# Moving the norm's squares on ScalarE and the last mixed group's activations on VectorE in a fused decoder layer

## The reference, cut to what matters

```python
h = h + jnp.concatenate([o_gdn, o_moba], axis=-1) @ w_o[i]
hn = rms_norm(h, ffn_norm[i])
h = h + (jax.nn.silu(hn @ w_gate[i]) * (hn @ w_up[i])) @ w_down[i]
```

## Time and profile before

| | us |
|---|---|
| median of 3 runs | 1311.7 |
| lowest and highest | 1311.44, 1312.51 |
| the profiled execution, its time | 1312.5 |
| the profiled execution, its span | 1310.8 |
| TensorE busy in it | 1302.5 |
| VectorE busy | 1025.2 |
| ScalarE busy | 704.7 |

### The profile page before, as it was taken

The page is one execution under the profiler, slowest core; times in us unless marked ns, Lnnn a source line. Parts: engine busy times, 40 slices in busy tenths (PEclk is TensorE's granted clock), DMA queues, the critical chain, the costliest instruction groups (busy, mean ns, idle before and its releaser), DMA issues.

```text
span 1310.8 us, 18558 instructions
## 1 busy us (share of the span) xinstructions
PE 1302.5 (99%) x6595; PEld 1076.9 (82%) x6595; DVE 1025.2 (78%) x1381; ACT 704.7 (54%) x937; POOL 53.7 (4%) x71
## 2 busy tenths in 40 slices
PE   9999999999999999999999999999999999999998
PEld 8788888887888887888888888888888888888887
DVE  6578886788586668889888988679888997968554
ACT  6576444543455565555555654445555555555643
POOL 4003000221000000000000000000000000000000
PEclk9999999999999999999999999999999999999999
DMA  8555554455434555665666556566666656556563
GB/s 271 177 174 164 159 147 129 145 149 152 144 119 145 177 177 164 205 211 184 194 198 207 192 193 216 185 211 184 198 205 209 190 182 209 193 178 208 193 199 139
DMA packets 126204, 238.37 MB, mean 182 GB/s; under 512 B 9711, under 2 KB 10786, under 8 KB 126138
## 3 DMA queue, kind: packets, MB, share of 16 engines
q1 hardware_dynamic: 126106, 237.48, 56.8%
q10 hardware_dynamic: 32, 0.01, 0.0%
HBM read 235.36 MB, written 2.10 MB: 181 GB/s over the span
## 4 chain that ended last, share of the span: by engine, by line
PE 98%; DVE 1%; ACT 0%; issue 0%; DMA 0%; DVEq 0%; ACTq 0%
PE pair L627 16%; PE pair L629 16%; PE pair L628 16%; PE pair L908 11%; PE pair L909 11%; PE pair L910 11%; PE bg L908 2%; PE bg L909 2%; PE bg L910 2%; PE bg L748 2%; PE bg L818 2%; PE bg L685 1%; PE bg L903 1%; PE bg L799 0%; PE bg L660 0%; DVE w_lo L1493 0%
## 5 line engine op out<-in xcount | busy, mean ns | idle before, releaser
L1493 DVE TENSOR_TENSOR w_lo<-raw,w_hi 128x1024 fp32r<-128x1024 f32 x442 | 531.8, 1222 | 179.2 <-ACT w_hi L1099 177.4
L1099 ACT ACTIVATE w_hi<-raw 128x1024 fp32r<-128x1024 f32 x401 | 417.1, 1055 | 250.5 <-PE pair L629 139.9
L627 PE MATMUL pair<-w_hi,xT_hi 128*128 128x512 f32 x780 | 314.6, 403 | 0.0
L629 PE MATMUL pair<-w_hi,xT_lo 128*128 128x512 f32 x780 | 305.0, 391 | 0.0
L628 PE MATMUL pair<-w_lo,xT_hi 128*128 128x512 f32 x780 | 304.4, 390 | 0.0
L629 PEld LDWEIGHTS pair<-w_hi,xT_lo 128*128 128x128 f32 x780 | 146.5, 188 | 31.5
L627 PEld LDWEIGHTS pair<-w_hi,xT_hi 128*128 128x128 f32 x780 | 146.9, 188 | 28.9
L628 PEld LDWEIGHTS pair<-w_lo,xT_hi 128*128 128x128 f32 x780 | 147.0, 188 | 27.4
L1373 ACT ACTIVATE w_hi<-raw 128x1024 fp32r<-128x1024 f32 x41 | 43.6, 1062 | 134.7 <-DVE raw L1823 134.7
L908 PE MATMUL pair<-w_hi,actT_hi 128*128 128x512 f32 x296 | 115.9, 392 | 0.0
L910 PE MATMUL pair<-w_hi,actT_lo 128*128 128x512 f32 x296 | 115.3, 389 | 0.0
(11 more groups left out here) (351 smaller groups left out, 1886.0 us busy)
## 6 DMA issues: line engine op xcount, KB each, us to landing
raw<-in_w_in_dram SPq DMA_DIRECT2D x112, 512.0 KB, 3.7
raw<-in_w_gate_dram SPq DMA_DIRECT2D x88, 512.0 KB, 4.6
raw<-in_w_up_dram SPq DMA_DIRECT2D x88, 512.0 KB, 4.5
raw<-in_w_down_dram SPq DMA_DIRECT2D x88, 512.0 KB, 4.8
raw<-in_w_o_dram SPq DMA_DIRECT2D x32, 512.0 KB, 3.9
raw<-in_w_ple_gate_dram SPq DMA_DIRECT2D x32, 512.0 KB, 4.1
raw<-in_w_ple_proj_dram SPq DMA_DIRECT2D x4, 512.0 KB, 4.1
h<-in_x_dram SPq DMA_DIRECT2D x3, 512.0 KB, 8.0
```

The source lines that it names most:

```text
L627: mm(banks[t][:], hi[:, ts], wh, start=first, stop=False)
L629: m = mm(banks[t][:], lo[:, ts], wh, start=False, stop=last)
L1099: f(w_hi[j % RING][:], raw[j % RING][:], ACT.Copy).then_inc(hi_ready, 1)
L1493: v.tensor_tensor(w_lo[j % RING][:], raw[j % RING][:], w_hi[j % RING][:].bitcast(F32), ALU.subtract).then_inc(lo_ready, 1)
```

## The change

`res_end` on ScalarE (the squares) is called later: for the first three `w_o` blocks two units into the next block, behind that step's `post("hA")`, and for the fourth block at step j = 3 of the first gate/up block, behind `post("hA", 7)`. ScalarE's rounding of group 7's forms is split off into `round_forms` and called at step j = 6; VectorE's whole part of group 7 (`post("hA", 7)`) is called at step j = 6 too, and behind it the sum of the squares. `res_end` loses its unused arguments. SyncE's, TensorE's and GpSimd's lists do not change.

```diff
--- before.py
+++ after.py
@@ -178,6 +178,7 @@
        + [("gate", MIXED[1]), ("up", MIXED[1])] + [("up", PLAIN[0])]
        + [("gate", MIXED[2]), ("up", MIXED[2])] + [("up", g) for g in PLAIN[1:]])
 assert len(SEQ) == 2 * UPB
+LAST_FORMS = SEQ.index(("up", MIXED[1])) - 2
 MIXED_END = SEQ.index(("up", MIXED[-1]))
 
 
@@ -1099,6 +1100,13 @@
                 f(w_hi[j % RING][:], raw[j % RING][:], ACT.Copy).then_inc(hi_ready, 1)
 
 
+            def round_forms(b, q):
+
+                act.wait_ge(form_ready, 4 * q + 1)
+                f(xT_hi[:, 2 * b, P:TOK], F_raw[:, 0, :], ACT.Copy)
+                act.wait_ge(form_ready, 4 * (q + 1))
+                f(F_hi[:, q, :, :], F_raw[:, 1:4, :], ACT.Copy).then_inc(form_rounded, 1)
+
             def post(step, b, half=None):
                 bk, i, use_n = where((step, b))
                 bh = heads(bk[:])
@@ -1136,10 +1144,8 @@
                         act.wait_ge(xg_ready, 2 * (q + 1))
                         f(xT_hi[:, 2 * b, 0:P], xg[:, 0, 0:P], ACT.Copy)
                         f(xT_hi[:, 2 * b + 1, :], xg[:, 1, :], ACT.Copy).then_inc(x_hi, 2)
-                        act.wait_ge(form_ready, 4 * q + 1)
-                        f(xT_hi[:, 2 * b, P:TOK], F_raw[:, 0, :], ACT.Copy)
-                        act.wait_ge(form_ready, 4 * (q + 1))
-                        f(F_hi[:, q, :, :], F_raw[:, 1:4, :], ACT.Copy).then_inc(form_rounded, 1)
+                        if b < UPB - 1:
+                            round_forms(b, q)
                         return
                     if step == "hA":
                         f(h1_raw[:], bk[:].rearrange("p (k t n) -> p k t n", k=2, t=NT)[:, :, 1, :], ACT.Copy).then_inc(h1_copied, 1)
@@ -1337,14 +1343,12 @@
                     f(mv[:, t, (b - 4) * CB:(b - 3) * CB], pair[n % 2][t][:], ACT.Copy,
                       scale=x_rs[:, t:t + 1]).then_inc(pair_free[n % 2], 1)
 
-            def res_end(last_unit, i, n):
-
-                wait_block(act, last_unit)
-                bno = (B_WO if i == 0 else B_DB) + n
-                wait_pair_read(act, bno)
+            def res_end(n):
+
+                wait_pair_read(act, B_WO + n)
                 for t in range(NT):
-                    f(junk[:], h[:, t, n * CB:(n + 1) * CB], ACT.Square, accum_out=h_ss[i][:, t, n:n + 1]).then_inc(h_sq, 1)
-                    act.wait_ge(h_sq, 8 * i + 2 * n + t + 1)
+                    f(junk[:], h[:, t, n * CB:(n + 1) * CB], ACT.Square, accum_out=h_ss[0][:, t, n:n + 1]).then_inc(h_sq, 1)
+                    act.wait_ge(h_sq, 2 * n + t + 1)
 
             for u in range(U_Z, U_GUA):
                 split(u + LEAD, u + LEAD)
@@ -1355,8 +1359,8 @@
                     z_end((u - U_Z) // UPB)
                 if U_WO - 2 * UPB <= u < U_WO and (u + 1 - U_MIX) % UPB == 0:
                     mix_end((u - U_MIX) // UPB)
-                elif U_WO <= u < U_GUA and (u + 1 - U_WO) % UPB == 0:
-                    res_end(u, 0, (u - U_WO) // UPB)
+                elif U_WO + UPB <= u and (u - U_WO) % UPB == 2:
+                    res_end((u - U_WO) // UPB - 1)
 
             def turned(n, kt):
 
@@ -1443,6 +1447,10 @@
                         for k in range(2):
                             for s in AT[u0 + j][k]:
                                 post(*s)
+                    if peeled and n0 == 0 and j == 3:
+                        res_end(3)
+                    if peeled and n0 == 0 and j == LAST_FORMS:
+                        round_forms(UPB - 1, len(MIXED) - 1)
                     if j == MIXED_END:
                         act.wait_ge(t_used, i * len(MIXED) + (m0 + len(MIXED)))
                         f(act_s[1][:], bg[0][:], ACT.Copy).then_inc(p1_copied, 1)
@@ -1783,16 +1791,12 @@
                     if n == 2 and j in (1, 5):
                         post("ba" if j == 1 else "gc", 0)
 
-            def res_end(last_unit, i, n):
+            def res_end(last_unit, n):
 
                 wait_block(dve, last_unit)
-                bno = (B_WO if i == 0 else B_DB) + n
                 for t in range(NT):
                     o = h[:, t, n * CB:(n + 1) * CB]
-                    v.tensor_tensor(o, o, pair[bno % 2][t][:], ALU.add).then_inc(pair_free[bno % 2], 1)
-                if n == 3:
-                    dve.wait_ge(h_sq, 8 * (i + 1))
-                    v.reduce_sum(h_s[i][:], h_ss[i][:], AX_X).then_inc(h_sum, 1)
+                    v.tensor_tensor(o, o, pair[(B_WO + n) % 2][t][:], ALU.add).then_inc(pair_free[(B_WO + n) % 2], 1)
 
             for u in range(U_Z, U_GUA):
                 split(u + LEAD, u + LEAD)
@@ -1802,7 +1806,7 @@
                 if u < U_MIX and (u + 1 - U_Z) % UPB == 0:
                     z_end((u - U_Z) // UPB)
                 if U_WO <= u < U_GUA and (u + 1 - U_WO) % UPB == 0:
-                    res_end(u, 0, (u - U_WO) // UPB)
+                    res_end(u, (u - U_WO) // UPB)
 
             def turned(n, kt):
                 for q in range(2):
@@ -1917,7 +1921,13 @@
                     if peeled:
                         for k in range(2):
                             for s in AT[u0 + j][k]:
-                                post(*s)
+                                if s != ("hA", UPB - 1):
+                                    post(*s)
+                    if peeled and n0 == 0 and j == LAST_FORMS:
+                        post("hA", UPB - 1)
+                    if peeled and n0 == 0 and j == 6:
+                        dve.wait_ge(h_sq, 8)
+                        v.reduce_sum(h_s[0][:], h_ss[0][:], AX_X).then_inc(h_sum, 1)
                     if j == MIXED_END:
                         p1 = act_s[1]
                         dve.wait_ge(p1_copied, i + (n0 + (2 if n0 else 0) + 1))
```

## The result

The median is 1314.47 us (22 runs, 1312.05 to 1315.53) against 1311.74 us before (22 runs on the same chips, 1310.95 to 1312.66). The ratio is 1.0019 with a 95% interval of 1.0013 to 1.0024: slower by 2.7 us. The interval leaves out 1, so the loss is real, and the bound of 0.2% lies inside it (by the two medians alone the difference is 0.21%). The profiled execution took 1314.79 us, with a span of 1313.1 us.

A forecast was written before the change was run, and what follows sets the result against it. TensorE was taken to bound the kernel, losing time only in a wait for VectorE's w_lo and a slow clock. From 1311.4, adding 1.49 + 0.2 and 0.9 of clock loss gave 1314.0 us, range 1311.6 to 1315.4.

The forecast's parts named there:

- the bound of 0.2%: Smallest difference that a measurement of this kernel was said to tell from no change: 2.6 us, upper limit 1314.3.
- block 4's squares: Ahead of G3, leaving lets G5's difference start 0.51 us earlier; ahead of G7's rounding, VectorE gets a new 2.0 us wait.
- the forms: Behind G9's w_lo they cost 2.68 us; G11's w_lo ends 1.49 later, TensorE waits 0.4 at G10, 2.5 at G11.
- 530.17: Time until which TensorE would have waited at G11 in the kernel before without a clock fall, 1.13 us before 531.30.
- 1.49 + 0.2: Time added without the clock: 1.49 us for the later w_lo of G11 and 0.2 for block 3.
- the clock's: Slow TensorE clock behind the wait ahead of G11: 0 to 1.7 us, taken as 0.9.
- 1311.4: Base of the sum: the kernel before without a clock fall, which is its fastest run.
- rival 1: Slower by over 0.2%: the clock falls fully behind the wait ahead of G11, 1314.8 us; chance 0.40.
- Block 3: Its moved squares delay the w_lo of G-2: 0.2 us taken, bounds nothing and 0.4.
- Behind the pairs: VectorE's lateness up to G15's w_lo has a cover of 0.3 us: costs nothing, at worst 0.2.
- Rival 2: Squares don't hold G7 up, G11's w_lo ends 0.5 us earlier: 1310.9 without, 1312.6 with clock loss; chance 0.11.
- Rival 3: Faster: w_lo of G8 and G11 come in time, all waits and the slow clock go, 1308.4 us; chance 0.07.

The follow-up runs named there:

- Run 1: Changed kernel with group 7's forms left between the w_lo of G6 and G7, so only the squares are moved: 1312.91 us.
- run 3: Changed kernel with block 4's squares one unit later, behind G7's rounding: 1312.99 us.
- run 2: Changed kernel with all squares back at the block ends as before, so only group 7's forms and their sum are moved: 1312.95 us.
- run 5: Kernel before with eight matmuls of unused product keeping TensorE busy in its wait ahead of G8: 1311.55 us.
- run 9: Changed kernel with the squares of blocks 1 to 3 back at the blocks' ends: 1314.27 us.
- run 7: Run 3 with group 6's transposes behind G0 instead of in the middle of G1: 1312.36 us.
- run 4: Changed kernel with nine matmuls of unused product keeping TensorE busy in its wait ahead of G11: 1313.25 us.
- run 6: Run 3 with the eight instructions of the last forms on GpSimd instead of VectorE: 1310.77 us.
- run 8: Run 3 with the last forms on GpSimd and group 6's transposes behind G0: 1311.20 us.
- run 10: Run 3 with the third mixed pair one plain unit later in every gate/up block, forms one step later: 1311.23 us.
- run 12: Run 6 with the third mixed pair one plain unit later in every gate/up block: 1310.69 us.

## Why the prediction was right, and where not

**The chain (steps on block 4's squares and on the forms).** Each position of the prediction stands in the trace, with 0.2 us of shift at the transposes: G5's difference 507.00 (said 506.8), ScalarE's rounding of G7 514.70 (514.53), its `w_lo` 515.80 (515.61) behind an idle time of 1.92 (2.0), G11's products 531.87 (531.66), waits of 1.04, 0.39 and 2.32 (1.2, 0.4 and 2.5). Run 1 and run 3 show that ScalarE's order makes the idle time: with the squares one unit later, 1.5 us are back. Runs 2 and 3 differ by 0.53 in the length of the chain (27.54 and 27.01), the 0.51 that the prediction gave to the squares' leaving the chain's start. One number of the working doesn't follow from its own rows: without the fall TensorE would have been due at G11 at 522.12 + 7.48 = 529.60 and not at 529.8. Nothing hangs on it, since both lie ahead of 530.17.

**What the forms' move does.** Run 3 has none of the squares' cost. Its chain is as long as that of run 5, the kernel before without its clock loss (27.01 and 27.04). What the squares' leaving the start wins, 0.5, the forms' leaving the place ahead of G7 costs again: in run 2 against run 5, both with the squares at the block's end, the chain is 0.50 longer (27.54 for 27.04). The forms cost their 2.68 us at either place, but their going frees only 2.19 between the `w_lo` of G6 and G7 (1.63 us apart in run 2, 3.82 in run 5), since VectorE idles there, 0.41 us in run 2, for a `w_hi` that ScalarE makes only behind group 7's `xT_hi`. So the move takes no work from VectorE; it takes the wait from G8 to G11. Yet run 3 is 1.27 above the kernel before (1312.99 against 1311.72). Its tail of 781.2 shows 1.6 of clock loss in the profiled execution. This is the point of the case: at G8 a fall of the clock ran in part into time that TensorE would have waited at G11 and cost 1.15 in the trace, and at G11 nothing is behind it that absorbs it, so it costs the whole 1.6. The fall also comes in more of the executions when the wait is at G11: a mean granted clock below 1.000 is recorded for 18 of 22 in the changed kernel and for 26 of 32 in runs 2, 3 and 9, but only for about half (50 of 93) in the sets of the kernel before. Why it comes more often there stays open.

**The sum.** In medians, with TensorE kept busy, the changed kernel is 1313.25 and the kernel before 1311.55: 1.70 between them, the prediction's 1.49 + 0.2. (That these agree to 0.01 is partly luck: the traces have 1.49 and 0.1.) The clock then adds 1.22 to the first and 0.19 to the second, which makes the 2.73 that were measured. The mis-sized term is the clock's: 0.9 taken, 1.2 measured; with it and with a base of 1311.55 in place of 1311.4 the time came out 0.5 above the forecast of 1314.0. The 0.9 stood for a part of a loss in each execution. What the executions show is nearer to a loss that comes whole or not at all: 4 of 22 have a clock of 1.000 and a median of 1313.5, the 18 below it one of 1314.7. The measured 1314.47 lies within the range of 1311.6 to 1315.4, but 0.2 us above the 1314.3 that the prediction set as the bound between its forecast and rival 1, and rival 1, the full clock loss, is at 1314.8 nearer to it than the forecast. The bound of 0.2% is too near for one of "within" and "over" to be called shown: the interval of 0.13 to 0.24% holds both. That the change stands within it by the ratio (0.19%) is luck; the path is what was right.

**The spread of before, and the base.** I read the spread of the three runs before as the clock. The mean granted clock recorded for each execution bears that out in the main. In the three sets of executions of the kernel before that were taken beside the experiments (33, 33 and 27), those at 1.000 have medians of 1311.26, 1311.20 and 1311.28, those at 0.998 or 0.999 have 1312.46, 1312.33 and 1312.55. The two groups are 1.1 to 1.3 apart, where the prediction worked out 1.13 for a full fall and the trace has 1.15 (28.19 - 27.04), and the base of 1311.4 is near the faster one. So the 0.19 that the median of before loses to the clock is not the price of a fall: about half of its executions have none. The clock is not the whole spread. In run 5, where TensorE is kept busy ahead of G8, it is still 1.99 us, and its executions at 0.999 are no slower than those at 1.000; where that rest comes from stays open.

**Small terms.** Block 3: 0.2 taken, 0.1 in the trace (run 9; the medians can't tell it from nothing), bounds 0 to 0.4. Behind the pairs: nothing taken, and the changed kernel's tail of 781.2 less the 1.6 of clock is within 0.1 of that of before, 779.5. Rival 2 (the squares don't hold G7 up) is shown wrong by run 3. Rival 3 (faster) is shown wrong by run 2: G8's wait went, and the backlog was still there at G11.

## What to carry to other kernels

A wait can be taken away and its reason left: look for the last instruction that the late engine owes before it has caught up, here G11's `w_lo` and not G8's. Small work on a second engine is free only until something that the late engine waits for is queued behind it; one unit further the same 1.5 us cost nothing. And where a wait lies matters as well as its length: here 0.55 of 1.70 us lost to a slow clock was absorbed by a further wait on the same late engine, and nothing where none followed. A median can hide such a loss when only a part of the executions has it, so look at the clock of each.

## What the hardware showed that I had not expected

- **Equal waits, unequal clocks.** Behind waits of 2.25 to 2.38 us the granted clock fell in the profiled executions of before, after and runs 1, 3 and 9, and did not in those of runs 2 and 7, whose waits are 2.31 and 2.32 us. Behind waits of 1.02 to 1.36 us (at G8 in after and runs 4 and 9, at G11 in runs 6 and 8, in the pair in run 10) it fell in none. The windows behind G11, of run 3 and then of run 2, show both levels:

```profile
530.28:533.70 3.42, 3.42 (x9) 2.75 (x10) 3.42 (x4) 2.83 (x3) 0.00 (x0) 0.59 0.83 287
```

```profile
530.80:534.20 3.40, 3.40 (x15) 2.83 (x16) 3.40 (x4) 2.76 (x3) 0.00 (x0) 1.00 0.86 280
```

  The first stretch holds 9 matmuls and the second 15. Beyond the traces, the mean granted clocks agree: none of the 66 executions of runs 4, 5, 6, 8, 10 and 12, whose waits are at most 1.36 us, has one of 0.998 (27 have 0.999), and 25 of the 76 of after and runs 1, 2, 3, 7 and 9 have. The Trainium skill (TensorE: Matmul & The Clock Gate, What's actually happening) says that the monitor runs on independently of the kernel; that is in line with a fall that comes in one execution and not in another, and no run here shows the monitor itself.
- **GpSimd slows VectorE.** In run 6 a `w_lo` of 1.22 us took 1.42, 1.48 and 1.96 beside GpSimd's subtractions, and a sum of 0.69 took 0.83 to 1.11. The Trainium skill (SBUF — State Buffer, Who interferes with whom) says that a VectorE instruction with two inputs in SBUF contends with one of GpSimd that reads SBUF. The trace agrees and adds the sizes.
